# The first scores of four attentions: each score, its filler, its exponential and its inverse in turn, with 12 filler chunks in the entry

## The reference

```
p = softmax(q k^T / 8)          # A: all 4 latent tiles and the cached context keys; context reads context
p = softmax([banded q k^T, sink])  # B: |i-j| <= 128 and the cached keys, with a learned sink logit per head
ya = (p v * silu(ga)) @ w_proj_a ; yb = ... ; yc = (spatial mix of branch C * silu(gc)) @ w_proj_c
y  = (sig_a * ya + sig_b * yb + sig_c * yc) @ w_out   # sig_r = sigmoid(h @ w_gate_r + b_gate_r)
x  = layer_norm(alpha * x + gate * y)
```

## Time and profile before

| | us |
|---|---|
| median of 3 runs | 1380.17 (1379.47 to 1381.62) |
| profiled execution, its own time | 1381.45 |
| its span, first to last instruction | 1379.6 |
| TensorE busy | 1350.9 (98%) |
| VectorE busy | 770.1 (56%) |
| GpSimd busy | 682.8 (49%) |
| ScalarE busy | 630.2 (46%) |

### The profile page before, as it was taken

How to read it: one execution, slowest core, us unless ns; L and a number is a source line. 1 busy time by engine, 2 the same in 40 slices (tenths; PEclk the granted TensorE clock), 3 DMA queues, 4 the chain that set the end, 5 groups by cost and what they waited for, 6 DMA issues and landing times.

```text
span 1379.6 us, 22530 instructions
## 1 busy us (share of the span) xinstructions
PE 1350.9 (98%) x8646; PEld 1256.8 (91%) x8646; DVE 770.1 (56%) x1634; ACT 630.2 (46%) x1330; POOL 682.8 (49%) x490
## 2 busy tenths in 40 slices
PE   7999999999999999999999999999999999999997
PEld 5898999899899999999888989998989989999986
DVE  5756773263883511655685577732468725036558
ACT  5446886244764221213264478843367733222130
POOL 3456565334665344344653666643356544445450
PEclk9999999999999999999999999999999999999999
DMA  9312001221013254354321220012120042125321
GB/s 376 131 62 81 16 31 47 77 81 62 32 47 123 76 174 151 104 209 134 132 105 42 74 76 31 32 47 80 62 77 31 32 138 77 61 77 199 126 88 77
DMA packets 36762, 126.88 MB, mean 92 GB/s; under 512 B 5040, under 2 KB 5808, under 8 KB 36656
## 3 DMA queue, kind: packets, MB, share of 16 engines
q1 hardware_dynamic: 29952, 108.54, 23.0%
q10 hardware_dynamic: 6704, 16.90, 3.4%
HBM read 119.66 MB, written 5.77 MB: 91 GB/s over the span
## 4 chain that ended last, share of the span: by engine, by line
PE 82%; DVE 4%; POOL 2%; ACT 2%; issue 1%; DVEq 0%; ACTq 0%; POOLq 0%
PE ps L996 30%; PE ps L981 17%; PE ps L925 6%; PE ps L927 6%; PE ps L926 6%; PE ps L1146 4%; PE ps L1159 2%; PE ps L1160 2%; PE ps L1136 2%; PE ps L1138 2%; POOL w_lo L1870 1%; DVE top L1721 1%; PE ps L1167 1%; PE ps L1013 1%; PE ps L1029 1%
## 5 line engine op out<-in xcount | busy, mean ns | idle before, releaser
L1870 POOL TENSOR_TENSOR w_lo<-raw,w_hi 128x1024 fp32r<-128x1024 f32 x148 | 360.1, 2440 | 269.3 <-ACT w_hi L1203 206.7
L1203 ACT ACTIVATE w_hi<-raw 128x1024 fp32r<-128x1024 f32 x148 | 154.1, 1054 | 151.4 <-DMA raw<-in_weights 65.9
L996 PE MATMUL ps<-h_hi,w_hi 128*128 128x320 f32 x736 | 170.2, 313 | 0.0
L981 PE MATMUL ps<-h_hi,w_hi 128*128 128x320 f32 x544 | 168.8, 310 | 0.2 <-DVE q_t L1690 0.2
L981 PE MATMUL ps<-h_hi,w_lo 128*128 128x320 f32 x544 | 168.2, 309 | 0.0
L981 PE MATMUL ps<-h_lo,w_hi 128*128 128x320 f32 x544 | 168.0, 309 | 0.0
L996 PE MATMUL ps<-h_hi,w_lo 128*128 128x320 f32 x736 | 168.0, 309 | 0.0
L996 PE MATMUL ps<-h_lo,w_hi 128*128 128x320 f32 x736 | 167.5, 309 | 0.0
L996 PEld LDWEIGHTS ps<-h_hi,w_hi 128*128 128x128 f32 x736 | 127.0, 189 | 11.2 <-issue 1.6
L925 PE MATMUL ps<-w_hi,h_hi 128*128 128x512 f32 (+1 forms) x360 | 129.2, 359 | 1.2 <-POOL w_lo L1870 1.0
L927 PE MATMUL ps<-w_hi,h_lo 128*128 128x512 f32 (+1 forms) x360 | 127.6, 354 | 0.0
(11 more groups left out here) (201 smaller groups left out, 3120.5 us busy)
## 6 DMA issues: line engine op xcount, KB each, us to landing
raw<-in_weights SPq DMA_DIRECT2D x190, 512.0 KB, 3.3
raw_more<-in_weights SPq DMA_DIRECT2D x10, 512.0 KB, 10.1
x<-in_x_sample ACTq DMA_DIRECT2D x6, 512.0 KB, 9.6
x_mid<-x ACTq DMA_DIRECT2D x5, 512.0 KB, 2.6
x<-x_mid ACTq DMA_DIRECT2D x5, 512.0 KB, 6.2
y_sample<-x SPq DMA_DIRECT2D x3, 512.0 KB, 2.6
pack<-in_pack ACTq DMA_DIRECT2D x2, 528.0 KB, 6.2
x<-in_x_sample SPq DMA_DIRECT2D x2, 512.0 KB, 5.1
```

Source lines behind the costliest of these rows:

```text
L981: last = pe.matmul(ps[:, s, 0:HALF], w[:, u % RING, first + k * P:first + (k + 1) * P], acts[:, k, half * HALF:(half + 1) * HALF], start=o ...
L996: last = pe.matmul(ps[:, s + half, 0:HALF], w[:, u % RING, cols], acts[:, k, half * HALF:(half + 1) * HALF], start=k == 0 and part == 0, s ...
L1203: did(act.activation(w_hi[:, n % RING, :], raw_tile(r), ACT.Copy), hi_made)
L1870: did(pool.tensor_tensor(w_lo[:, n % RING, :], raw_tile(r), w_hi[:, n % RING, :], ALU.subtract), w_ready)
```

## The change

In the entry, each score is now followed by its share of filler, then by its own exponential and inverse, and only then comes the next score. The entry's filler grows to 12 chunks. In A it was 8 chunks, of which one stood ahead of the first score; now three stand ahead of it in layer 0 and one in layer 1. In B it was 9 chunks, one of them ahead of the first score; now all 12 are behind the first score. The total filler stays, so the steps of A get 39 chunks where they had 43, and the steps of B get 39 where they had 42.

```diff
-def attention(l, br, first_filler, filler, last_filler, lag, ahead):
+def attention(l, br, ahead_filler, first_filler, filler, last_filler, lag, ahead):
...
+    out.extend(ahead_filler)
     for i, e in enumerate(scores[-1]):
+        out.append(e)
         out.extend(first_filler[len(first_filler) * i // len(scores[-1]):len(first_filler) * (i + 1) // len(scores[-1])])
-        out.append(e)
-        if i:
-            out.append(exps[-1][i - 1])
-            out.extend(v for v in inverses[-1] if v[1:] == scores[-1][i - 1][1:])
-    out.append(exps[-1][-1])
-    out.extend(v for v in inverses[-1] if v[1:] == scores[-1][-1][1:])
+        out.append(exps[-1][i])
+        out.extend(v for v in inverses[-1] if v[1:] == e[1:])
...
-    steps = list(flat(attention(l, "a", filler[:8], filler[8:-5], filler[-5:], 2, 3)))
+    begun = 3 if l == 0 else 1
+    steps = list(flat(attention(l, "a", filler[:begun], filler[begun:12], filler[12:-5], filler[-5:], 2, 3)))
...
-    out.extend(flat(attention(l, "b", filler[:9], filler[9:-3], filler[-3:], 2, 3)))
+    out.extend(flat(attention(l, "b", [], filler[:12], filler[12:-3], filler[-3:], 2, 3)))
```

## The result

| | before | after |
|---|---|---|
| median, us | 1380.75 (4 runs, 1379.47 to 1381.62) | 1399.15 (4 runs, 1398.50 to 1399.74) |
| ratio | | 1.0129, 95% interval 1.0116 to 1.0141 |
| profiled execution, its own time and span | 1381.45, 1379.6 | 1398.50, 1396.6 |
| TensorE busy, us | 1350.9 | 1353.8 |
| mean granted clock | 0.997 | 0.996 |

The change makes the kernel 18.4 us slower by the medians and 17.05 us by the two profiled executions. The forecast was +10.3, to 1390.5, with a range from 1383 to 1396: the sign is right, the size isn't, and the time lies outside the range.

What follows compares the result with a forecast made beforehand. TensorE, busy 1350.9 of 1379.6 us, was taken as the bound, so only its waits and clock could change. Terms -0.5 + 2.2 + 4.3 + 4.3 gave +10.3, forecast 1390.5 us, range 1383 to 1396.

Steps and rivals of the forecast that it cites:

- A0: Layer 0's attention A: keys' wait and clock dip vanish, new chain and step waits come; 4.2 against 4.7 us, -0.5.
- A1: Layer 1's attention A: the serial chain falls behind and new waits come; 4.7 against 2.5 us, +2.2.
- the B's: Attention B of each layer: late chain and shifted gate ends make TensorE wait; +4.3 us each.
- 8.2: Each attention B after the change: us of waits laid by hand in entry and steps, set against 4.1 before.
- 4.5: Each attention B before the change: us the same hand laying gives, where the trace has 4.1.
- the last one nothing: Steps of A that come 0.88 us early without a chunk: waits of 0.7 and 0.4 us, none at the last.
- 2.54 us for each unit in a row: Entry of A: time from one maximum to the next once score, exponential and inverse stand in turn.
- The keys' wait and the dip: Layer 0's A: 1.53 us wait before the first score and 1.7 us of lower clock near 118 us both vanish.
- the third rival: The clock falls at the new waits: two to four dips add 3.4 to 6.8 us, 1394 to 1397; chance 0.14.
- Rival one: The chunks cover the chain: twelve chunks hide every unit, -8.2 us, 1372.0; chance 0.07.
- Only the entries change: Rival: the steps absorb their missing chunks and the entries alone count; +0.8 us, 1381; chance 0.12.
- What was to show it: Signs in the trace: gate wait of 1.5 to 2 us in A1, maxima 2.5 us apart, no lower clock near 118.

Runs made afterwards that it cites:

- Only the B's: The kernel of before with the change's order and chunk amounts in both attentions B alone, the A's left as before: 1392.14 us, ratio 1.0082.
- Fill, exp in turn: The changed kernel with each inverse moved behind the next score, chunk amounts and exponentials in turn kept: 1394.56 us, ratio 1.0093.
- fill only: The kernel of before with the change's chunk amounts but the old order of scores, exponentials and inverses: 1398.22 us, ratio 1.0121.
- after again: The changed kernel, the same program measured once more with nothing altered: 1400.44 us, ratio 1.0138.
- order only: The kernel of before with the change's order but the old chunk amounts, 8 in A entries and 9 in B: 1393.21 us, ratio 1.0087.
- best: Two kernels against before: inverse one score behind, exponentials ahead of chunks in B's steps, 9 to 11 entry chunks: 1375.11 and 1374.79 us.

## Why the prediction missed

The sum was -0.5 (A0) + 2.2 (A1) + 4.3 + 4.3 (the B's) = 10.3. The trace gives +17.2 from start to start, 6.9 more.

- **The term of the B's failed, +4.3 where 5.9 was lost; 3.2 of the 6.9 us.** The mechanism laid was right, but it was one of two. Of the waits laid by hand, 1.5, 0.55, 1.3, 1.05, 0.85 and 2.0 came as 1.33, 0.43, 1.09, 1.29, 0.62 and 1.79, and group 7's 0.95 as 0.17 and 0.42. Group 6 was laid at nothing and waits 0.75. The prediction counted missing chunks as cover for the A's only; for the B's it took them as a shift of the gates' ends, and group 6 is where a step lost its cover. By the prediction's own rule a bracket is some 0.15 us short from start to start, so nine brackets with 7.9 us in them make 9.2, not 8.2, and 0.9 of that difference is group 6.

  The subtraction is wrong too: 8.2 holds waits alone, and the 4.1 it was set against holds small gaps as well (the three brackets of before make 3.0 from start to start). With 4.1 before, 5.9 more is 10.0, so some 0.8 us of small gaps were left out of the 8.2. And the 4.3 follows from neither pair of the text's numbers: 8.2 - 4.1 is 4.1 and 8.2 - 4.5 is 3.7. "Only the B's" gives 5.9 in each B, with no dip to blur it.
- **A1 failed by size, +2.2 for +3.0.** The new wait at the gate's first chunk was 1.73 for 1.9, the first PV 1.06 for 1.3. The steps waited 0.83, 0.29 and 0.53 us where I had laid 0.7, 0.4 and nothing. From start to start that is 2.1 for 1.1 and more than the whole 0.8: the step that failed is above all "the last one nothing". 2.54 us for each unit in a row held to 0.02. "Fill, exp in turn" shows that the loss is 1.0 when the inverse alone is moved back behind the next score; "fill only" shows that the old order loses 3.0 as well, so against the old order, which the change replaced, the serial order costs A1 nothing at these amounts.
- **A0, -0.5 for +0.3.** The keys' wait and the dip went, as forecast; the dip was worth 1.6 for the 1.7 taken. That it went with the wait was in part luck, since "only the B's" keeps the wait and has no dip. The waits that replaced them were 0.52, 1.17 and 0.39 in the entry, less than laid, and 0.82, 0.29 and 0.54 in the steps, again more than the 1.1 laid there.
- **The clock.** The forecast let it gain 1.7 in A0 and lose nothing. In the profiled execution of after it cost 0.6 in B0 and most of 1.2 in the head; with 0.2 between A0 and A1 that closes the 6.9. In B0 the stretch of 3.4 us costs only 6.5 - 5.9 = 0.6, because the wait of 0.75 at group 6, which B1 shows, is absent there: a TensorE that is late by more than a wait does not wait. TensorE's waits in after, B0 and then B1:

```profile
PE ps L1135 <- ACT p_f_b L1362: 5.4, 6, 1.8
```

```profile
PE ps L1135 <- ACT p_f_b L1362: 6.1, 7, 1.8
```

  In "fill only" a dip in B0 costs 7.9 - 6.3 = 1.6. The executions of after have mean clocks of 0.995 and 0.996, those of "after again" 0.994 three times of four, those of before 0.995 to 0.998. So the third rival, held at 0.14, was half true. Of the seven profiled executions whose B's have 12 or 14 chunks in the entry, six show at least one dip in a B; of the other seven none does. The dips are worth some 1.8 of the 6.9 us that the sum missed, not the whole miss. (The prediction counts seven new waits over 1.2 us; its own list has nine.) The Trainium skill (TensorE: Matmul & The Clock Gate, A second HAM failure mode: psum-queue depth-cycling) tells of a kernel in which frequent short idles between groups of matmuls made the clock swing between both levels. The traces of after agree, with two and four stretches of 3.4 us in some 1397 us. "Only the B's", with the same waits in its B's, shows none in its profile, and two of its four executions have the mean clock of 0.999. The price is that of the rows here, not a rate from the page.
- **The chunks do not cover the chain.** Rival one falls, by "order only" and by the unit of 2.54 us. **Only the entries change** falls too: from group 2 on, B1's brackets hold 6.1 us where they held 1.4 before.
- **What was to show it** came as written: 1.73 us at the gate's matmul with the gate's copy as releaser, no wait at the first T of A1 and of the B's, maxima 2.5 us apart, 1.33 at B's third T, 1.79 at a score of group 5 and no lower clock at 118 us. One sign of being wrong came too, a lower clock in several stretches. Such a list tests a mechanism and not its sum.

What stays open: whether the dips at 26 us have to do with the changed programs at all. Six of the fourteen profiled executions show one there, with the same code; "only the B's", "fill only" and both "best" have none. How much of a B's 5.9 us is the gates' ends and how much the missing cover was not measured apart. And the gaps too small for a bracket, some 0.8 us of a B, were not traced to an operation.

## What to carry to other kernels

Where a queue is served in order, filler is not only an amount. Taking chunks out of a step moves the end of a gate against the exponentials, and a copy that waits for TensorE then holds back an exponential that TensorE waits for; a step that loses its chunk can also uncover the chain between two scores. Count the whole attention's waits, not the entry's, and subtract like from like: waits laid from waits measured, not from a total that holds small gaps too. An operation that depends on another engine is better placed one unit behind its producer (the inverse behind the next score) than right behind it: with after's amounts that alone was worth 4.6 us between the medians, 1399.15 and 1394.56, of which the traces show 2.1 us in each A. Where waits of one microsecond and more are added, put the clock's price beside them.

## What the runs showed of the hardware

- A stretch of 3.4 us at a granted clock of 0.50 to 0.53 cost 1.2 to 1.6 us where nothing behind it waits less (A0 of "only the B's" -1.6; A1 and B1 of "after, again" 4.2 - 3.0 and 7.4 - 5.9), but 0.6 where it took the place of a later wait.
- One program's executions differ by it: "only the B's" took 1391.04 to 1394.79 us at mean clocks of 0.999 to 0.996. A single profiled execution therefore can't settle an effect below some 4 us of this kernel; measuring by parts, start to start, does, to about 0.1 us where the part has no such stretch: parts that an edit left alone differ by 0.0 to 0.1 us.
- ScalarE's queue stood idle for 3.05 us behind a copy whose bank TensorE had not filled, with an exponential behind it that TensorE then waited for, 1.79 us.
